# U with one 512-column matmul for a key's high part, halves summed on VectorE, and a quarter of the low parts on GpSimd

## Chip, cores and metric

One core of one Trainium2 chip runs the whole kernel. The metric is device microseconds of one execution. The profile is one further execution, taken with the hardware profiler; its span runs from the first to the last instruction.

## The reference

One decoder layer in fp32 for 256 tokens of width 1024: a mixer, cross-attention, and then the PEER channel mixer, which this change is about. Cut to that:

```python
q = (t @ w_q).reshape(T, PEER_HEADS, 2, PEER_HALF)
s = jnp.einsum('thpd,hpnd->thpn', q, sub_keys)
s_top, i_top = lax.top_k(s, PEER_TOPK)
...
best_s, pos = lax.top_k(cand_s, PEER_TOPK)
ids = jnp.take_along_axis(cand_i, pos, axis=-1)
gates = jax.nn.softmax(best_s, axis=-1)
...
act = jax.nn.gelu(jnp.einsum('td,ted->te', x_c, u[ids_c]), approximate=False)
return jnp.einsum('te,ted->td', g_c * act, v[ids_c])
```

There are 128 x 128 experts. The kernel does not gather rows of u and v. It computes gelu(x u) for every expert, multiplies by a routing matrix that is zero outside the chosen ones, and multiplies by all of v.

## The kernel before

**Precision.** fp32 operands are split in two fp32r parts: the high part is a copy of the value into fp32r (made by ScalarE, ACT), the low part is the value minus the high part (made by VectorE, DVE). A product is then three matmuls: high x high, high x low and low x high.

**Stages.** The mixer and cross-attention run to about 298 us. The U stage runs over 128 keys; for one key j the product of 128 experts (rows) with 256 tokens is made, over 8 chunks of 128 of the model width. That is 24 matmuls of 256 columns a key (L1214 to L1216), into `bank[k][:, 0:T]` with k = j % 4. Then come the routing stage (groups of 4 tokens, L1243 on TensorE) and the V stage (L1262, 512-column matmuls, 12 a key).

**Buffers of U.** `raw` holds two halves of two keys each; SP loads a half (1 MB, L261) once DVE has made the low parts of both its keys (`s_ul`). `hl`, `hl2` and `hl3u` are four slots for the high and low parts, one for each k. The tokens' high and low parts lie side by side in `xt[:, c, 0]` and `xt[:, c, 1]`. There are four PSUM banks, one for each k.

**Order of the U stage.** Each engine has its own queue, written by hand, and goes through it in order.
- TensorE (PE): key j waits for its low part (`s_ul`) and for the gelu of key j-4, which frees its bank (`s_ua`).
- ACT, in a loop of 8 keys: `gelu(j)` reads the bank and writes `act_w[:, j]` (L581); then `split_high` (L577) makes the high part of key j+4, once PE is done with key j and the data has landed.
- DVE, written out without a loop: `split_low` (L886) for key j+4, and then, for some keys, one `route_pass`. A route pass is a quarter of the top-16 search for one of 16 pairs of token tile and head: parts 0 and 1 find the best 16 of 128 scores (L902 to L910), part 2 the best 16 of 256 candidates (L912, L902 to L906), part 3 turns positions to indices (L917 to L926). There are 64 of them, spread by `5 * (j + 1) // 8 > parts`, which gives 5 in 8 keys.
- GpSimd (POOL) does nothing in U. Its subtraction of 128x2048 in two earlier weight units (L312) and its work in the routing stage (L320, L327) are the places where it runs beside DVE.
- At the end, inside the last four keys, PE transposes the routing rows `krow` (L1222) into the unused half of banks 0 to 2 and ACT copies each to `kt3` (L607), from which routing starts.

## Time and profile before

| | us |
|---|---|
| median of 3 runs | 1159.22 |
| lowest and highest | 1153.96, 1159.23 |
| span of the profiled execution | 1152.3 |
| U stage in it, first to last matmul | 300.6 to 670.4 |
| routing stage | 670.4 to 798 |
| V stage | 798 to 1146.6 |

No own time of the profiled execution is given beside its span; the median is 6.9 us longer than the span. The time of an engine's instruction can be read in two ways: its duration, and the step from its start to the start of the next one in the queue, which is shorter where the next one had nothing to wait for.

### The profile page before, as it was taken

The page shows a single profiled execution, that of the slowest core. Times are in us where ns is not written, and L with a number is a line of the kernel's source. Part 1 is how long each engine was busy: PE and PEld are TensorE (multiplying, and loading weights), DVE is VectorE, ACT ScalarE, POOL GpSimd, SP SyncE. Part 2 cuts the span into 40 slices and gives each one's busy share as a digit, 9 for nine tenths or more (in the row PEclk, how much of TensorE's full clock was granted, in tenths as well). Part 3 has the DMA queues.
Part 4 walks back from the last instruction along what each step waited for, and adds up shares of the span by engine and source line. Part 5 has one row for each costly group of instructions (what it writes and reads, how often), then busy time and mean ns, then how long its engine had stood idle before and what let it go on. Part 6 is the DMA issues. An engine that isn't in the chain of part 4 may idle for free.

```text
span 1152.3 us, 20363 instructions
## 1 busy us (share of the span) xinstructions
PE 1085.2 (94%) x7278; PEld 1002.3 (87%) x7278; DVE 786.0 (68%) x1333; ACT 621.2 (54%) x1034; POOL 120.7 (10%) x101
## 2 busy tenths in 40 slices
PE   7999999989999999999999976667999999999998
PEld 6988999889899999999999975656888888888886
DVE  5774674453488889888884489998555555555554
ACT  6775555453555555555555576665545545455453
POOL 0000110010000000000000067884000000000000
PEclk9999999999999999999999988898999999999999
DMA  9544345252355454555445520001555555555552
GB/s 318 167 149 145 111 167 163 74 183 110 112 181 184 180 184 180 182 184 182 183 180 185 185 86 0 0 0 36 188 204 191 185 198 200 182 191 207 184 187 105
DMA packets 60658, 179.54 MB, mean 156 GB/s; under 512 B 4048, under 2 KB 42960, under 8 KB 44112
## 3 DMA queue, kind: packets, MB, share of 16 engines
q1 hardware_dynamic: 60624, 179.09, 44.7%
q8 instruction: 21, 0.34, 0.1%
q14 instruction: 13, 0.11, 0.0%
HBM read 178.03 MB, written 1.05 MB: 155 GB/s over the span
## 4 chain that ended last, share of the span: by engine, by line
PE 48%; issue 40%; DVE 7%; ACT 2%; POOL 2%; DMA 1%; DVEq 0%; POOLq 0%; SPq 0%; ACTq 0%
PE acc L1262 30%; PE acc L1044 13%; PE bank L1243 2%; DVE act_w L968 2%; DVE oh_i L957 2%; DVE oh_j L957 1%; POOL oh_i L320 1%; ACT wsp L347 1%; DVE wsp L663 1%; DMA wraw<-w_in 1%; PE bank L1148 0%; PE bank L1126 0%; POOL sqd L327 0%; PE bank L1073 0%; POOL wsp L312 0%
## 5 line engine op out<-in xcount | busy, mean ns | idle before, releaser
L886 DVE TENSOR_TENSOR hl<-raw,hl 128x1024 fp32r<-128x1024 f32 x192 | 234.4, 1225 | 170.0 <-ACT hl L577 168.2
L577 ACT ACTIVATE hl<-raw 128x1024 fp32r<-128x1024 f32 x192 | 202.6, 1056 | 135.7 <-PE acc L1262 126.3
L1262 PE MATMUL acc<-hl,whl 128*128 128x512 f32 x1152 | 266.6, 389 | 1.8 <-DVE whl L985 1.8
L1262 PEld LDWEIGHTS acc<-hl,whl 128*128 128x128 f32 x1152 | 216.3, 188 | 46.6 <-issue 1.9
L1214 PE MATMUL bank<-xt,hl 128*128 128x256 f32 x768 | 218.1, 284 | 0.0
L1215 PE MATMUL bank<-xt,hl 128*128 128x256 f32 x768 | 217.5, 283 | 0.0
L1216 PE MATMUL bank<-xt,hl 128*128 128x256 f32 x768 | 217.5, 283 | 0.0
L1214 PEld LDWEIGHTS bank<-xt,hl 128*128 128x128 f32 x768 | 147.5, 192 | 0.3 <-DVE hl L886 0.3
L1215 PEld LDWEIGHTS bank<-xt,hl 128*128 128x128 f32 x768 | 147.6, 192 | 0.2 <-issue 0.2
L1216 PEld LDWEIGHTS bank<-xt,hl 128*128 128x128 f32 x768 | 147.5, 192 | 0.0
L663 DVE TENSOR_TENSOR wsp<-wraw,wsp 128x2048 fp32r<-128x2048 f32 x35 | 80.2, 2290 | 73.9 <-ACT wsp L347 73.7
L581 ACT ACTIVATE act_w<-bank 128x256 f32 (+1 forms) x128 | 48.9, 382 | 144.4 <-PE bank L1216 139.9
L1243 PE MATMUL bank<-oh_j,oh_i 128*128 128x128 f32 x512 | 86.2, 330 | 39.8 <-POOL oh_i L320 39.7
L1044 PE MATMUL acc<-xt,wsp 128*128 128x256 f32 x960 | 119.0, 287 | 3.5 <-DVE xt L684 3.5
L1044 PEld LDWEIGHTS acc<-xt,wsp 128*128 128x128 f32 x960 | 117.6, 194 | 4.5 <-issue 4.3
L1243 PEld LDWEIGHTS bank<-oh_j,oh_i 128*128 128x128 f32 x512 | 77.2, 234 | 48.7 <-issue 38.9
L347 ACT ACTIVATE wsp<-wraw 128x2048 fp32r<-128x2048 f32 x35 | 66.9, 1913 | 81.8 <-PE acc L1044 81.8
L1262 PE MATMUL acc<-hl3v,whl 128*128 128x512 f32 x384 | 92.4, 389 | 0.0
L1262 PEld LDWEIGHTS acc<-hl3v,whl 128*128 128x128 f32 x384 | 72.1, 188 | 14.9
L320 POOL TENSOR_TENSOR oh_i<-oh_i,kt 128x512 f32<-128x512 f32 x64 | 80.7, 1271 | 22.3 <-DVE oh_i L957 22.3
L1214 PE MATMUL bank<-xt,hl3u 128*128 128x256 f32 x256 | 72.6, 284 | 0.0
L1215 PE MATMUL bank<-xt,hl3u 128*128 128x256 f32 x256 | 72.5, 283 | 0.0
(207 smaller groups left out, 1448.3 us busy)
## 6 DMA issues: line engine op xcount, KB each, us to landing
raw<-u_t SPq DMA_DIRECT2D x64, 1024.0 KB, 4.8
raw<-v SPq DMA_DIRECT2D x64, 1024.0 KB, 4.7
wraw<-w_in SPq DMA_DIRECT2D x9, 1024.0 KB, 8.0
wraw<-w_pq SPq DMA_DIRECT2D x8, 1024.0 KB, 5.2
wraw<-w_ck SPq DMA_DIRECT2D x4, 1024.0 KB, 5.0
wraw<-w_cv SPq DMA_DIRECT2D x4, 1024.0 KB, 4.9
wraw<-w_out SPq DMA_DIRECT2D x4, 1024.0 KB, 4.9
wraw<-w_cq SPq DMA_DIRECT2D x4, 1024.0 KB, 5.0
```

What stands on the lines that cost most here:

```text
L320: nc.gpsimd.tensor_tensor(oh_i(slot), oh_i(slot), kt3[:, 2, ds(t0, GRP)].unsqueeze(2).broadcast_to([P, GRP, P]), ALU.mult).then_inc(s_gi, 1)
L347: nc.scalar.activation(wsp[:, u % 2, 0], wraw[:, u % WRAW], ACT.Copy).then_inc(s_wh, 1)
L577: nc.scalar.activation(eslot(k, 0, second), raw[:, k // 2, k % 2], ACT.Copy).then_inc(ready, 1)
L581: nc.scalar.activation(act_w[:, ds(j, 1)].rearrange("p o t -> p (o t)"), bank[k % 4][:, 0:T], ACT.Gelu).then_inc(s_ua, 1)
L663: V.tensor_tensor(wsp[:, u % 2, 1], wraw[:, u % WRAW], wsp[:, u % 2, 0].bitcast(F32), ALU.subtract).then_inc(s_wl, 1)
L886: V.tensor_tensor(eslot(k, 1, second), raw[:, k // 2, k % 2], eslot(k, 0, second).bitcast(F32), ALU.subtract).then_inc(ready, 1)
L1044: last = pe.matmul(dst, a, b, start=(c == c0 and n == 0), stop=(c == c1 - 1 and n == 2))
L1214: pe.matmul(bank[k][:, 0:T], uh[:, c], xt[:, c, 0], start=(c == 0), stop=False)
L1215: pe.matmul(bank[k][:, 0:T], uh[:, c], xt[:, c, 1], start=False, stop=False)
L1216: last = pe.matmul(bank[k][:, 0:T], ul[:, c], xt[:, c, 0], start=False, stop=(c == DC - 1))
L1243: last = pe.matmul(bank[slot][:, P * k:P * k + P], oh_i(slot)[:, k], oh_j(slot)[:, k], start=True, stop=True)
L1262: last = pe.matmul(acc[:, 2 * t + n], a, b[:, 512 * n:512 * n + 512], start=False, stop=last_key and k == 2, skip_group_check=True)
```

## The change

Four things.
- PE: in place of two 256-column matmuls with the same weights (high part of the key against the tokens' high part, then their low part), one matmul of 512 columns takes both (`xt[:, c]` is contiguous). The low part of the key still meets the tokens' high part in 256 columns. A key has 16 matmuls.
- The two halves of the bank must be added. ACT copies the right half to `act_w[:, j]` (`half_out`), DVE adds the left half to it (`u_sum`), and ACT makes the gelu for two keys at once in SBUF (`gelu_pair`, 512 columns). A bank is free after `u_sum` (`s_us`).
- The low part of every key with k = 3 is made by POOL (`u_low`, `s_ulp`); DVE makes the other three. SP waits for both before it loads the half of keys 2 and 3. Route passes are spread 3 in 5 keys.
- The whole bank is in use, so the transposes of `krow` and the copies to `kt3` now follow after the last key.

```diff
--- before.py
+++ after.py
@@ -172,6 +172,7 @@
         s_oi, s_gi, s_dif, s_ojd, s_oja, s_sqd, s_gm, s_gw = (sem(n) for n in (
             "s_onehot_i", "s_gated_i", "s_differences", "s_onehot_j_dve", "s_onehot_j_act", "s_sq_distance", "s_route_mm", "s_route_mul"))
         s_seed = sem("s_seed")
+        s_us, s_u2, s_ulp, s_kt = sem("s_u_sum"), sem("s_u_half_out"), sem("s_u_low_pool"), sem("s_key_cols_mm")
         s_vh, s_vl, s_Wh, s_Wl, s_vm = (sem(n) for n in ("s_v_high", "s_v_low", "s_a_high", "s_a_low", "s_v_mm"))
         s_fs, s_fv, s_fd, s_fin = (sem(n) for n in ("s_fin_squares", "s_fin_var", "s_fin_dev", "s_fin"))
 
@@ -257,10 +258,14 @@
                 sp.dma_start(raw[:, q], u_t[q]).then_inc(s_raw[q], 16)
             with sp.Fori(1, KEYS // 4) as it:
                 for q in range(2):
-                    sp.wait_ge(s_ul, it * 4 - 4 + 2 * q + 2)
+                    sp.wait_ge(s_ul, it * 3 - 3 + q + 2)
+                    if q:
+                        sp.wait_ge(s_ulp, it)
                     sp.dma_start(raw[:, q], u_t[ds(it * 2 + q, 1)].rearrange("o p j d -> (o p) j d")).then_inc(s_raw[q], 16)
             for q in range(2):
-                sp.wait_ge(s_ul, KEYS - 4 + 2 * q + 2)
+                sp.wait_ge(s_ul, 3 * (KEYS // 4) - 1 + q)
+                if q:
+                    sp.wait_ge(s_ulp, KEYS // 4)
                 sp.dma_start(raw[:, q], vd[q]).then_inc(s_raw[q], 16)
             sp.wait_ge(s_um, KEYS)
             sp.dma_start(gfin[:], g_final.rearrange("(o d) -> o d", o=1).broadcast_to([P, D])).then_inc(s_gf, 16)
@@ -312,6 +317,15 @@
                 nc.gpsimd.tensor_tensor(wsp[:, u % 2, 1], wraw[:, u % WRAW], wsp[:, u % 2, 0].bitcast(F32),
                                         ALU.subtract).then_inc(s_wlp, 1)
 
+
+            def u_low(n):
+                pool.wait_ge(s_uh, n)
+                nc.gpsimd.tensor_tensor(eslot(3, 1, False), raw[:, 1, 1], eslot(3, 0, False).bitcast(F32),
+                                        ALU.subtract).then_inc(s_ulp, 1)
+
+            u_low(4)
+            with pool.Fori(1, KEYS // 4) as it:
+                u_low(it * 4 + 4)
 
             pool.wait_ge(s_kte, 3)
 
@@ -576,35 +590,45 @@
                     act.wait_ge(*free)
                 nc.scalar.activation(eslot(k, 0, second), raw[:, k // 2, k % 2], ACT.Copy).then_inc(ready, 1)
 
-            def gelu(j, k):
+            def half_out(j, k):
                 act.wait_ge(s_um, j + 1)
-                nc.scalar.activation(act_w[:, ds(j, 1)].rearrange("p o t -> p (o t)"), bank[k % 4][:, 0:T], ACT.Gelu).then_inc(s_ua, 1)
+                nc.scalar.activation(act_w[:, ds(j, 1)].rearrange("p o t -> p (o t)"), bank[k % 4][:, T:2 * T],
+                                     ACT.Copy).then_inc(s_u2, 1)
+
+            def gelu_pair(j):
+                act.wait_ge(s_us, j + 2)
+                aw = act_w[:, ds(j, 2)]
+                nc.scalar.activation(aw, aw, ACT.Gelu).then_inc(s_ua, 1)
 
             act.wait_ge(s_pv, HEADS + CHEADS)
             for k in range(4):
                 split_high(k, 16 if k % 2 == 0 else None, (s_seed, 1) if k == 2 else None, s_uh)
             base16 = 16 * (KEYS // 4)
 
-            with act.Fori(0, KEYS // JPB - 1) as it:
+            for it in range(KEYS // JPB - 1):
                 for jj in range(JPB):
                     j = it * JPB + jj
                     if jj == JPB - 1:
                         act.wait_ge(s_rt, it + 1)
-                    gelu(j, jj)
-
+                    half_out(j, jj)
                     split_high(jj % 4, (it * 2 + (jj // 4 + 2)) * 16 if jj % 2 == 0 else None, (s_um, j + 1), s_uh)
+                    if jj % 2:
+                        gelu_pair(j - 1)
 
             act.wait_ge(s_rt, TT * PH)
             nc.scalar.activation(krow[:, 2], krow[:, 2], ACT.Exp).then_inc(s_ge, 1)
             for jj in range(JPB):
                 j = KEYS - JPB + jj
+                half_out(j, jj)
                 if jj < 4:
                     split_high(jj, base16 if jj % 2 == 0 else None, (s_um, j + 1), s_uh)
                 elif jj < 7:
                     split_high(jj - 4, base16 + 16 if jj % 2 == 0 else None, (s_um, j + 1), s_vh, second=True)
-                gelu(j, jj)
-                if 4 <= jj < 7:
-                    nc.scalar.activation(kt3[:, jj - 4], bank[jj - 4][:, T:2 * T], ACT.Copy).then_inc(s_kte, 1)
+                if jj % 2:
+                    gelu_pair(j - 1)
+            for k in range(3):
+                act.wait_ge(s_kt, k + 1)
+                nc.scalar.activation(kt3[:, k], bank[k][:, T:2 * T], ACT.Copy).then_inc(s_kte, 1)
 
 
             def onehots(it, n, g, t0, slot, first):
@@ -925,18 +949,23 @@
                     rlink(V.tensor_reduce(kr[:, 0:2, ds(it, 1)].rearrange("p a o k -> p a (o k)"), eq[:], X, ALU.add))
                     V.tensor_scalar(kr[:, 2, ds(it, 1)], topv[:, 2:3], topv[:, 2, 0:1], None, ALU.subtract).then_inc(s_rt, 1)
 
-            for k in range(4):
+            def u_sum(j):
+                dve.wait_ge(s_u2, j + 1)
+                V.tensor_tensor(act_w[:, j], bank[j % 4][:, 0:T], act_w[:, j], ALU.add).then_inc(s_us, 1)
+
+            for k in range(3):
                 split_low(k, s_ul, (s_uh, k + 1))
             dve.wait_ge(s_ke, 8)
 
 
             parts = 0
-            for j in range(KEYS - 1):
-                if j < KEYS - 4:
+            for j in range(KEYS):
+                u_sum(j)
+                if j < KEYS - 4 and j % 4 < 3:
                     split_low(j % 4, s_ul, (s_uh, j + 5))
-                else:
+                elif KEYS - 4 <= j < KEYS - 1:
                     split_low(j % 4, s_vl, (s_vh, j + 5 - KEYS), second=True)
-                if parts < 4 * TT * PH and 5 * (j + 1) // 8 > parts:
+                if parts < 4 * TT * PH and 3 * (j + 1) // 5 > parts:
                     route_pass(parts // 4, parts % 4)
                     parts += 1
                 if j == KEYS - JPB:
@@ -1201,33 +1230,35 @@
             last.then_inc(s_seed, 1)
 
 
-            def u_keys(it, first=False, last_pass=False):
+            def u_keys(it, first=False):
                 for k in range(4):
-                    pe.wait_ge(s_ul, it * 4 + (k + 1))
+                    if k < 3:
+                        pe.wait_ge(s_ul, it * 3 + (k + 1))
+                    else:
+                        pe.wait_ge(s_ulp, it + 1)
                     if first:
                         pe.wait_ge(s_ke, 5 + k)
                     else:
-                        pe.wait_ge(s_ua, it * 4 + (k - 3))
+                        pe.wait_ge(s_us, it * 4 + (k - 3))
                     uh = eslot(k, 0, False).rearrange("p (c i) -> p c i", c=DC)
                     ul = eslot(k, 1, False).rearrange("p (c i) -> p c i", c=DC)
                     for c in range(DC):
-                        pe.matmul(bank[k][:, 0:T], uh[:, c], xt[:, c, 0], start=(c == 0), stop=False)
-                        pe.matmul(bank[k][:, 0:T], uh[:, c], xt[:, c, 1], start=False, stop=False)
+                        pe.matmul(bank[k][:], uh[:, c], xt[:, c].rearrange("p a t -> p (a t)"), start=(c == 0), stop=False)
                         last = pe.matmul(bank[k][:, 0:T], ul[:, c], xt[:, c, 0], start=False, stop=(c == DC - 1))
-                    if last_pass and k < 3:
-
-                        if k == 0:
-                            pe.wait_ge(s_gr, 1)
-                        for t in range(TT):
-                            last = pe.transpose(bank[k][:, T + P * t:T + P * t + P], krow[:, k, t], ident[:])
                     last.then_inc(s_um, 1)
 
             u_keys(0, first=True)
-            with pe.Fori(1, KEYS // 4 - 1) as it:
+            with pe.Fori(1, KEYS // 4) as it:
                 u_keys(it)
-            u_keys(KEYS // 4 - 1, last_pass=True)
-
-            pe.wait_ge(s_ua, KEYS)
+
+            pe.wait_ge(s_gr, 1)
+            for k in range(3):
+                pe.wait_ge(s_us, KEYS - 3 + k)
+                for t in range(TT):
+                    last = pe.transpose(bank[k][:, T + P * t:T + P * t + P], krow[:, k, t], ident[:])
+                last.then_inc(s_kt, 1)
+
+            pe.wait_ge(s_ua, KEYS // 2)
             pe.wait_ge(s_kte, 3)
 
             def route(it, slot, first=False):
```

Where the new instructions stand, by the program's order. DVE, soon after the start of U (keys 4 to 6 before, 5 to 8 now). `hl`, `hl_54` and `hl3u` are the slots of the parts (L886 before, L910 now), `act_w<-bank` is the new sum, the rest are route passes. Before:

```order
L886 TENSOR_TENSOR hl<-raw,hl 128x1024
L912 TENSOR_TENSOR cand<-topv 128x256
L902 MAX topv<-cand 128x8
L903 MATCH_REPLACE candw<-topv,cand 128x256
L904 MAX topv<-candw 128x8
L905 MAX_INDEX topi<-topv,cand 128x8
L906 MAX_INDEX topi<-topv,candw 128x8
L886 TENSOR_TENSOR hl<-raw,hl 128x1024
L886 TENSOR_TENSOR hl_54<-raw,hl_54 128x1024
L917 TENSOR_SCALAR posu<-topi 128x16
```

DVE's queue now:

```order
L954 TENSOR_TENSOR act_w<-bank,act_w 128x256
L910 TENSOR_TENSOR hl<-raw,hl 128x1024
L954 TENSOR_TENSOR act_w<-bank,act_w 128x256
L910 TENSOR_TENSOR hl_54<-raw,hl_54 128x1024
L941 TENSOR_SCALAR posu<-topi 128x16
L942 TENSOR_SCALAR posu<-topi 128x16
L943 CAST posf<-posu 128x32
L944 TENSOR_TENSOR eq<-posf,iota 128x512
L947 TENSOR_TENSOR eq<-eq,topf 128x512
L949 TENSOR_REDUCE krow<-eq 128x2x16
L950 TENSOR_SCALAR krow<-topv 128x16
L954 TENSOR_TENSOR act_w<-bank,act_w 128x256 x2
```

Each key now has a sum ahead of its split, and where the key's slot is the fourth and no route pass falls on it, two sums follow each other.

ACT's queue over four keys late in U, now (L595 is the copy of the right half, L591 the high part, L601 the gelu of two keys). Before, it was L581 and L577 in turn, one of each for a key.

```order
L595 ACTIVATE act_w<-bank 128x256
L591 ACTIVATE hl<-raw 128x1024
L595 ACTIVATE act_w<-bank 128x256
L591 ACTIVATE hl<-raw 128x1024
L601 ACTIVATE act_w<-act_w 128x512
```

The gelu of two keys waits for DVE's sum, and stands ahead of the next key's copy and high part.

ACT at the end of U, before:

```order
L581 ACTIVATE act_w<-bank 128x256
L607 ACTIVATE kt_65<-bank 128x256
L581 ACTIVATE act_w<-bank 128x256
L616 ACTIVATE sqd_66<-sqd_66 128x512
L621 ACTIVATE oh_j_70<-sqd_66,ones 128x512
```

and now, where the three copies to `kt3` have moved behind the last gelu:

```order
L595 ACTIVATE act_w<-bank 128x256
L601 ACTIVATE act_w<-act_w 128x512
L631 ACTIVATE kt_65<-bank 128x256 x3
L640 ACTIVATE sqd_66<-sqd_66 128x512
L645 ACTIVATE oh_j_70<-sqd_66,ones 128x512
```

## Rows read from the trace of the kernel before

**Rows 1.** The page, 40 equal slices of the span: DVE's busy tenths.
```profile
DVE  5774674453488889888884489998555555555554
```

**Rows 2.** Busy time by stretch: length, PE, PEld, DVE, ACT, POOL (count), granted clock, DMA.
```profile
300.60:670.40 369.80, 369.80 (x3080) 369.40 (x3078) 294.65 (x678) 193.98 (x277) 1.08 (x1) 1.00 0.51 182
400.00:500.00 100.00, 100.00 (x836) 100.00 (x835) 87.68 (x217) 50.90 (x74) 0.00 (x0) 1.00 0.52 184
682.00:798.00 116.00, 77.80 (x470) 69.45 (x469) 115.01 (x135) 73.17 (x171) 91.44 (x72) 0.87 0.00 0
```

**Rows 3.** Who waited for whom from 400 to 600 us: total, times, longest.
```profile
ACT act_w L581 <- PE bank L1216: 84.3, 61, 1.6
DVE hl L886 <- ACT hl L577: 7.8, 15, 1.3
```

**Rows 4.** The chain that ended last, its piece in V: start, us, what.
```profile
798.16 348.43 PE acc L1262 x1536
```

**Rows 5.** DVE in order of time: start, duration, line, operation, [idle before].
```profile
447.78 0.42 DVE L912 TENSOR_TENSOR cand<-topv 128x256 f32<-128x256 f32 x1
...
450.60 1.23 DVE L886 TENSOR_TENSOR hl<-raw,hl 128x1024 fp32r<-128x1024 f32 x1
...
453.54 0.17 DVE L917 TENSOR_SCALAR posu<-topi 128x16 uint32<-128x16 uint32 x1
...
454.04 0.69 DVE L920 TENSOR_TENSOR eq<-posf,iota 128x512 f32<-128x512 f32 x1
454.76 0.69 DVE L923 TENSOR_TENSOR eq<-eq,topf 128x512 f32<-128x512 f32 x1
...
456.35 1.22 DVE L886 TENSOR_TENSOR hl<-raw,hl 128x1024 fp32r<-128x1024 f32 x1
457.49 0.28 DVE L902 MAX8 topv<-srow 128x8 f32<-128x128 f32 x1
...
459.39 1.22 DVE L886 TENSOR_TENSOR hl<-raw,hl 128x1024 fp32r<-128x1024 f32 x1
```

**Rows 6.** DVE before 240 us, two adds of a PSUM and an SBUF operand in succession.
```profile
231.33 0.76 DVE L831 TENSOR_TENSOR xr<-acc,xr 128x256 f32<-128x256 f32 x2 [1.46 <-PE acc L1044]
```

**Rows 7.** ACT in order of time, in U.
```profile
456.80 0.39 ACT L581 ACTIVATE act_w<-bank 128x256 f32 x1 [1.55 <-PE bank L1216]
457.08 1.05 ACT L577 ACTIVATE hl<-raw 128x1024 fp32r<-128x1024 f32 x1
459.68 0.39 ACT L581 ACTIVATE act_w<-bank 128x256 f32 x1 [1.55 <-PE bank L1216]
```

**Rows 8.** All instructions in order of time, where POOL's L312 runs beside DVE.
```profile
165.28 4.60 POOL L312 TENSOR_TENSOR wsp<-wraw,wsp 128x2048 fp32r<-128x2048 f32 x1 [24.18 <-ACT wsp L347]
...
166.67 3.75 DVE L679 TENSOR_SCALAR xs<-xr,stat 128x1024 f32<-128x1024 f32 x1
```

**Rows 9.** Single lines: duration min/median/max in ns, first and last start, form.
```profile
L679 DVE TENSOR_SCALAR xs<-xr,stat x6: 753/754/3752, 5.9 to 240.3; 128x1024 f32<-128x1024 f32 x6
```

**Rows 10.** The same view, one of DVE's lines in the routing stage, beside POOL.
```profile
L957 DVE TENSOR_TENSOR oh_i<-iota,kt x64: 678/1140/1553, 669.9 to 792.4; 128x512 f32<-128x512 f32 x64
```

**Rows 11.** The same view, POOL's line in the routing stage.
```profile
L320 POOL TENSOR_TENSOR oh_i<-oh_i,kt x64: 1034/1452/1487, 671.6 to 793.6; 128x512 f32<-128x512 f32 x64
```

**Rows 12.** The page, DMA issues: count, KB each, median us to landing.
```profile
raw<-u_t SPq DMA_DIRECT2D x64, 1024.0 KB, 4.8
```

**Rows 13.** The end of U in order of time: POOL.
```profile
669.32 1.54 POOL L327 TENSOR_TENSOR sqd<-kt,iota 128x512 f32<-128x512 f32 x1 [431.34 <-ACT kt L607]
```

**Rows 14.** The same stretch, DVE.
```profile
669.88 5.02 DVE L957 TENSOR_TENSOR oh_i<-iota,kt 128x512 f32<-128x512 f32 x4
```

**Rows 15.** The same stretch, ACT.
```profile
668.87 0.38 ACT L607 ACTIVATE kt<-bank 128x256 f32<-128x256 f32 x1
670.45 0.38 ACT L581 ACTIVATE act_w<-bank 128x256 f32<-128x256 f32 x1 [1.21 <-PE bank L1216]
670.95 0.63 ACT L616 ACTIVATE sqd<-sqd 128x512 f32<-128x512 f32 x1
```

## The prediction, made before the changed kernel was run

> **What bounds the kernel now.** First the chain of waits and the busy shares by stretch. In the U stage (369.8 us, a third of the span) TensorE (PE) is busy without a gap at a granted clock of 1.00, its upper level of 2.4 GHz [rows 2]. The waits say the same from the other side: of the waits in 200 us of U, ScalarE (ACT) waits 84.3 us for PE, VectorE (DVE) 7.8 us for ACT, and PE waits for nobody [rows 3]. ACT starts a gelu every 2.88 us, once a key, each time after 1.55 us of waiting for PE [rows 7]. So U lasts 128 keys of PE: 369.5 / 128 = 2.887 us a key, 24 matmuls, 120.3 ns each.
>
> Then see who is next. DVE is at 88% between 400 and 500 us [rows 2] and at 8 tenths in most slices of U [rows 1]. Its queue, in steps from start to start [rows 5]: a split takes 1.14 us (456.35 to 457.49), route parts 0 and 1 1.90 us (457.49 to 459.39), part 2 2.82 (447.78 to 450.60), part 3 2.81 (453.54 to 456.35). A round of four parts is 9.43 us. Per 20 keys that is 20 x 1.14 + 12.5 x 9.43/4 = 22.8 + 29.5 = 52.3 us of 57.7. DVE hides behind PE with 5 us in 58 to spare. After routing ends, at about key 102, DVE has room.
>
> **PE's part.** The V stage shows what a 512-column matmul costs: 348.43 us for 1536 of them [rows 4], 226.8 ns. Against two of 256 columns, 240.6 ns, it saves 13.8 ns. A key becomes 8 x (226.8 + 120.3) = 2.777 us, U becomes 355.5 us: **14.0 us less**, if nothing but PE sets the pace. Both ends: at the least nothing is saved (a 512 followed by a 256 in other weights does not occur in the trace), and no row supports more than 14. I take 14, since both kinds run back to back at the full clock and show the same 13 to 14 ns over their columns at 2.4 GHz.
>
> On this the Trainium skill's page VectorE: DVE Perf Modes (section The TRN2 errata) differs: it gives a matmul 6 cycles over its columns, 2.5 ns, by which the 1024 matmuls fewer would be worth an estimated 2.6 us. The rows here disagree with that figure by a factor of five, and the rows are used.
>
> **DVE's part.** Removed: 5 of 20 splits, 5.7 us. The route spread of 3 in 5 gives 12 parts in 20 keys, 28.3 us. Added: 20 sums of a PSUM half and an SBUF row. The nearest row adds the same operands in the same shape: two in 0.76 us, each 0.42 with a step of 0.34 [rows 6]. Taken at 0.34: 6.8 us; at 0.42 it would be 8.4. The sum: 17.1 + 28.3 + 6.8 = **52.2 us in 20 keys, where PE now needs 55.5**. The reserve falls from 5.4 to 3.3 us. Two things eat it.
>
> *The handshake with ACT.* `gelu_pair` of an odd key waits for DVE's sum and stands ahead of the next key's copy and high part. While PE sets the pace this is free. Once DVE is late, each odd key makes DVE wait for ACT: 0.1 for the signal, 0.53 for a gelu of 512 (the nearest row, a 512-element SBUF square, takes 0.63 [rows 15]), 0.38 for the copy and 0.1: the next sum can start 1.1 us after the last, and the next split at 0.1 + 0.53 + 0.28 + 1.05 + 0.1 = 2.06 us [rows 7]. Where a route pass stands between, it hides that. In 20 keys the odd ones without a pass are 5, 7, 15 and 17. At 5 and 17 DVE has a split (1.14) and a sum (0.34) to do and waits 0.6; at 7 and 15, where the split has gone to POOL, it waits 1.1 and then 0.6. Together **4.6 us**.
>
> *The port.* POOL now reads and writes SBUF during U. The trace shows what this does to DVE. L312 on POOL takes from 165.28 to 169.88; a DVE instruction started at 166.67 takes 3.75 us and ends at 170.42, 0.54 us after POOL's [rows 8], where the same line takes 0.75 alone [rows 9]. It was held until POOL was through. Instructions with two SBUF operands are held too: L957 takes 0.68 alone, 1.14 in the median and 1.55 at most in the routing stage, and POOL's own L320 goes from 1.03 to 1.45 [rows 10, 11]. A split, the cand of part 2 and both eq of part 3 have two SBUF operands; the sum has one.
>
> The Trainium skill, SBUF — State Buffer (section Who interferes with whom), states this as an exclusive lock: a DVE instruction with two SBUF inputs and a GpSimd one that reads SBUF block each other for the whole instruction. The trace agrees, by the 3.75 us.
>
> A low part of 1024 on POOL, by 4.60 us for 2048 and 1.03 for 512 [rows 8, 11], takes 1.03 + (4.60 - 1.03)/3 = 2.2 us. Five of them in 20 keys can hold DVE for 0 to 11 us. To see how much, I wrote the queues of 20 keys out, with these durations and DVE late. One of the five as an example: ACT has the high part for key 11's slot ready just as DVE, behind with its work, begins part 3 for key 6; POOL takes the port 0.2 us into it, the first eq is due 0.3 us later and waits for the rest of POOL's 2.2 us, 1.9 us, and everything behind it in DVE's queue moves by as much. The five fall so: ahead of a split, but there DVE is first (0.2 us lost, at a cast); just at the start of part 3, both eq wait (1.9); after a split and ahead of part 2, whose cand waits (1.9); behind part 3, the next split waits (1.4); inside a cand (0). Together **5.4 us**, half of the most.
>
> **The sum.** DVE late, 20 keys take 52.2 + 4.6 + 5.4 = 62.2 us, against 57.7 before and 55.5 for PE. So PE comes to wait for DVE's low parts. Through key 106, with the last route part (2.8 us) off the path: 107/20 x 62.2 - 2.8 = 330.0. Plus 4 us for the first dozen keys, where DVE has nothing to fall behind on and waits as it does now (12% of 2.9 us a key, and the first sum only behind key 0). Then PE does keys 110 to 127 at its own pace, 18 x 2.777 = 50.0. U is 384.0, **14.5 more than 369.5**.
>
> *The tail.* Before, the copies to `kt3` lay inside the last keys (the last at 668.87), POOL started routing at 669.32 and DVE at 669.88, ahead of PE's end at 670.4 [rows 13 to 15]. Now DVE's first one-hot waits for the half copy (0.5 after PE), the sum (0.4), the gelu (0.6) and the first of three copies (0.5): 2.0 after PE's end instead of 0.5 ahead. POOL's start moves by about 3.5. DVE is busy 99% of routing [rows 2], so its shift is what counts: **+2.7** (1.5 to 3.5). V is not touched.
>
> *At nothing:* ACT's table load, one a loop turn before, is now rare, and ACT has 1.55 us a key idle (costs nothing unless ACT becomes late). ACT's added work: a copy for a gelu, and half a gelu of 512, 0.3 us a key. SP's load of the second half waits for POOL: POOL's end, landing 4.8 [rows 12], two high parts and a copy, 2.2 of POOL make 10.4 us per 4 keys, under the 11.1 of PE's pace; held by a split it is 11.5, still under the 12.4 above.
>
> Total: 1152.3 + 14.5 + 2.7 = 1169.5 us of span; with the 6.9 us that the median stands above the profiled span, **1176 us, 1.5% slower**.
>
> **The rivals.**
> 1. *PE stays the bound (faster).* If DVE is held little, since POOL starts when ACT finishes a high part and DVE, being on time, is in a sum or a maximum then. 52.2 + 4.6 = 56.8 in 20 keys is then hardly above PE's 55.5. U 355.5 to 358, tail 2.7: 1148 to 1151 us. For: the reserve of 3.3, and an on-time DVE splits key 4 only after POOL's 2.2 us are over. Against: once a part 3 or a cand meets POOL, 2 us are lost, and the handshake keeps it late.
> 2. *Halfway.* Each us of port loss in 20 keys is worth 107/20 = 5.35 in the total. Even with before is U = 369.5 - 2.7 = 366.8, so (366.8 - 50.0 - 4 + 2.8)/5.35 = 59.0 for 20 keys, a loss of 2.2 us. That is the point from which the change is slower. Losses of 1.1 to 3.3 us give 1153 to 1165.
> 3. *Port dearer.* A loss of 8 us or more, as when each POOL instruction stands before a split: 5.35 x 2.6 = 14 more, 1190 and up. Also if the sum costs 0.42 with a gap each: +8.
> 4. *The 512-column matmul doesn't save:* by itself +14 on rival 1, so 1162; under my forecast DVE sets the pace and only the last 18 keys lose 2 us.
>
> **How the numbers follow.** A measurement here tells 0.5% (5.8 us) from no change. My forecast, 1165 to 1188: 0.52. Rival 1 (with up to 1.1 us of port loss, to 1153): 0.24. Rivals 2 and 4: 0.14. Rival 3: 0.10. The time is the forecast's, 1176. The range reaches to 1149 and 1190, leaving out the lowest of rival 1 and most of rival 3. Faster 0.24, same 0.14, slower 0.62.
>
> **What would show it.** Right: PE waits in U for L910 or L323, about 10% of the time up to key 110, DVE at 95% or more with splits and eq lasting up to 3 us where POOL runs, ACT waiting for the sum at L601, and a pace of 3.0 to 3.1 us a key that falls to 2.78 after routing. Wrong: PE without gaps at 2.78 us a key (rival 1), splits of 1.2 us beside POOL (no port), or a sum of well over 0.4 us. A granted clock under 1.00 in U, from PE's waits, would add what none of these sums has.

## The result: slower by 2.7%, and the profile after

The changed kernel takes 1188.23 us in the median of 4 runs (1184.45 to 1190.87), the kernel before 1158.19 (1153.96 to 1159.23). The ratio is 1.0267, with a 95% interval of 1.023 to 1.0304. The profiled execution took 1190.61 us, with a span of 1188.7. One of the six executions in experiment 9 below took 1224.87 us at a mean granted clock of 0.839, against 0.975 to 0.985 in the other five, and its ratio leaves it out.

The stages by the trace: U runs from 304.0 to 704.1 us, that is 400.1 us, where it was 369.6 (both to the last matmul's start plus its 0.12 us; the 369.8 of the table ahead goes to its modelled end). Routing and the gap ahead of V take 130.4 us (704.1 to 834.5) where they took 127.9. From V's first matmul to the end of the span it is 354.2 us, as before.

The page of the changed kernel, DVE and POOL by slices, with the granted clock. It answers to [rows 1].

```profile
DVE  5775674442688999999999569999555555555554
POOL 0000010000121121112112138887000000000000
PEclk9989999999999999999999998889999999999999
```

DVE was at 8 tenths in most slices of U and is now at 9, where POOL shows its 1 or 2 tenths. Busy time by stretch (length, PE, PEld, DVE, ACT, POOL, clock, DMA) answers to [rows 2]:

```profile
400.00:500.00 100.00, 91.58 (x495) 77.64 (x494) 90.95 (x216) 47.25 (x78) 19.43 (x8) 0.97 0.44 158
```

PE was busy all the time and is now idle 8% of it. Who waited for whom from 400 to 600 us answers to [rows 3]:

```profile
ACT act_w L601 <- DVE act_w L954: 102.6, 31, 5.8
PEld bank L1246 <- issue: 24.2, 21, 2.8
PE bank L1246 <- DVE hl L910: 14.5, 13, 2.5
DVE hl L910 <- ACT hl L591: 5.8, 12, 0.5
DVE act_w L954 <- ACT act_w L595: 5.8, 6, 1.0
```

ACT used to wait for PE; it now waits for DVE's sum, half of the time (102.6 us of 200). PE waits for DVE's low parts; part of PE's waiting stands under "issue", since the profile finds no releaser for it. DVE waits for ACT in 11.6 us of 200. DVE sets the pace, together with its waits for ACT.

What happens in its queue is in DVE's order of time:

```profile
441.57 0.42 DVE L954 TENSOR_TENSOR act_w<-bank,act_w 128x256 f32<-128x256 f32 x1
441.91 3.35 DVE L910 TENSOR_TENSOR hl<-raw,hl 128x1024 fp32r<-128x1024 f32 x1
445.19 0.41 DVE L954 TENSOR_TENSOR act_w<-bank,act_w 128x256 f32<-128x256 f32 x1
...
455.48 2.27 DVE L943 CAST posf<-posu 128x32 f32<-128x32 uint32 x1
457.78 0.69 DVE L944 TENSOR_TENSOR eq<-posf,iota 128x512 f32<-128x512 f32 x1
...
460.10 0.42 DVE L954 TENSOR_TENSOR act_w<-bank,act_w 128x256 f32<-128x256 f32 x1
461.49 0.42 DVE L954 TENSOR_TENSOR act_w<-bank,act_w 128x256 f32<-128x256 f32 x1 [0.97 <-ACT act_w L595]
462.44 1.23 DVE L910 TENSOR_TENSOR hl<-raw,hl 128x1024 fp32r<-128x1024 f32 x1 [0.52 <-ACT hl L591]
...
469.20 3.33 DVE L910 TENSOR_TENSOR hl<-raw,hl 128x1024 fp32r<-128x1024 f32 x1
...
481.70 3.34 DVE L910 TENSOR_TENSOR hl<-raw,hl 128x1024 fp32r<-128x1024 f32 x1
```

and POOL's, a little further on:

```profile
441.79 2.39 POOL L323 TENSOR_TENSOR hl3u<-raw,hl3u 128x1024 fp32r<-128x1024 f32 x1 [8.36 <-ACT hl3u L591]
455.32 2.38 POOL L323 TENSOR_TENSOR hl3u<-raw,hl3u 128x1024 fp32r<-128x1024 f32 x1 [11.14 <-ACT hl3u L591]
469.09 2.37 POOL L323 TENSOR_TENSOR hl3u<-raw,hl3u 128x1024 fp32r<-128x1024 f32 x1 [11.38 <-ACT hl3u L591]
481.56 2.40 POOL L323 TENSOR_TENSOR hl3u<-raw,hl3u 128x1024 fp32r<-128x1024 f32 x1 [10.10 <-ACT hl3u L591]
495.87 2.56 POOL L323 TENSOR_TENSOR hl3u<-raw,hl3u 128x1024 fp32r<-128x1024 f32 x1 [11.90 <-ACT hl3u L591]
506.79 2.40 POOL L323 TENSOR_TENSOR hl3u<-raw,hl3u 128x1024 fp32r<-128x1024 f32 x1 [8.37 <-ACT hl3u L591]
```

POOL started at 441.79, 0.12 us ahead of DVE's split. The split lasts 3.35 us where it takes 1.22, and ends 1.08 us after POOL's 444.18, about its own length. A cast of 32 elements lasts 2.27 us where it takes 0.18 (455.48). The pattern repeats after 65.0 us (441.79, 506.79), that is 20 keys: 3.25 us a key, where PE needed 2.887 before. Over these 65.0 us: 52.2 us of DVE's work, three splits held 2.1 us each (441.91, 469.20, 481.70) and one cast 2.1, together 8.4, and 3.9 us of waiting for ACT (0.97 twice, 0.52 twice, 0.45 twice). That makes 64.5.

The end of U, in DVE's and ACT's order of time, answers to [rows 14, 15]:

```profile
706.14 4.18 DVE L986 TENSOR_TENSOR oh_i<-iota,kt 128x512 f32<-128x512 f32 x4 [0.97 <-ACT kt L631]
```

```profile
705.21 0.63 ACT L601 ACTIVATE act_w<-act_w 128x512 f32<-128x512 f32 x1 [0.49 <-DVE act_w L954]
705.74 0.91 ACT L631 ACTIVATE kt<-bank 128x256 f32<-128x256 f32 x3
```

DVE starts routing 2.0 us after PE's end at 704.1; it started 0.5 us ahead of it.

### The profile page after: what moved, and what is told of

Same layout as the page of the kernel before. It is cut to its first block, busy times and chain, and to the rows that moved or that the text cites. A ratio compares the mean times of both kernels' runs of the same rounds, so it can differ in the third digit from the quotient of the medians.

```text
span 1188.7 us, 18325 instructions
## 1 busy us (share of the span) xinstructions
PE 1091.1 (92%) x6254; PEld 952.3 (80%) x6254; DVE 833.8 (70%) x1429; ACT 631.7 (53%) x1084; POOL 198.3 (17%) x133
## 4 chain that ended last, share of the span: by engine, by line
PE 47%; issue 41%; DVE 7%; ACT 2%; POOL 2%; DMA 1%; DVEq 0%; POOLq 0%; SPq 0%; ACTq 0%
PE acc L1293 29%; PE acc L1073 12%; PE bank L1274 2%; DVE act_w L997 2%; DVE oh_i L986 2%; DVE oh_j L986 1%; ACT wsp L361 1%; DMA wraw<-w_in 1%; POOL oh_i L334 1%; DVE wsp L687 1%; PE bank L1177 0%; PE bank L1155 0%; PE bank L1102 0%; POOL wsp L317 0%; DVE xs L703 0%
## 5 line engine op out<-in xcount | busy, mean ns | idle before, releaser
L910 DVE TENSOR_TENSOR hl<-raw,hl 128x1024 fp32r<-128x1024 f32 x192 | 262.8, 1369 | 148.7 <-ACT hl L591 148.7
L1246 PE MATMUL bank<-xt,hl 128*128 128x512 f32 x768 | 280.4, 406 | 21.3 <-DVE hl L910 20.7
L591 ACT ACTIVATE hl<-raw 128x1024 fp32r<-128x1024 f32 x192 | 202.8, 1057 | 133.7 <-PE acc L1293 126.2
L1247 PE MATMUL bank<-xt,hl 128*128 128x256 f32 x768 | 218.1, 284 | 0.0
L1246 PEld LDWEIGHTS bank<-xt,hl 128*128 128x128 f32 x768 | 147.0, 191 | 64.2 <-issue 29.7
L1247 PEld LDWEIGHTS bank<-xt,hl 128*128 128x128 f32 x768 | 147.9, 193 | 0.2 <-issue 0.2
L323 POOL TENSOR_TENSOR hl3u<-raw,hl3u 128x1024 fp32r<-128x1024 f32 x32 | 77.8, 2430 | 378.9 <-ACT hl3u L591 378.9
L601 ACT ACTIVATE act_w<-act_w 128x512 f32<-128x512 f32 x64 | 40.4, 632 | 167.7 <-DVE act_w L954 167.7
L1246 PE MATMUL bank<-xt,hl3u 128*128 128x512 f32 x256 | 91.6, 398 | 5.0 <-DVE act_w L954 5.0
L954 DVE TENSOR_TENSOR act_w<-bank,act_w 128x256 f32<-128x256 f32 x128 | 53.9, 421 | 26.0 <-ACT act_w L595 24.3
L1247 PE MATMUL bank<-xt,hl3u 128*128 128x256 f32 x256 | 71.7, 280 | 0.0
```

The costliest lines, as they stand in the source:

```text
L323: nc.gpsimd.tensor_tensor(eslot(3, 1, False), raw[:, 1, 1], eslot(3, 0, False).bitcast(F32), ALU.subtract).then_inc(s_ulp, 1)
L591: nc.scalar.activation(eslot(k, 0, second), raw[:, k // 2, k % 2], ACT.Copy).then_inc(ready, 1)
L910: V.tensor_tensor(eslot(k, 1, second), raw[:, k // 2, k % 2], eslot(k, 0, second).bitcast(F32), ALU.subtract).then_inc(ready, 1)
L954: V.tensor_tensor(act_w[:, j], bank[j % 4][:, 0:T], act_w[:, j], ALU.add).then_inc(s_us, 1)
L1246: pe.matmul(bank[k][:], uh[:, c], xt[:, c].rearrange("p a t -> p (a t)"), start=(c == 0), stop=False)
L1247: last = pe.matmul(bank[k][:, 0:T], ul[:, c], xt[:, c, 0], start=False, stop=(c == DC - 1))
```

## The experiments

In all of them the pace is read from the distance of route passes or low parts that are 20 keys apart in the steady part of U. The lines of code differ from kernel to kernel by a few numbers. The ratios are to the kernel before, which was run again beside each group of experiments (medians 1157.4 to 1158.5 us).

**1. DVE makes all low parts.** POOL's `u_low` and its waits are out, PE and SP wait for `s_ul` alone:

```diff
-                if j < KEYS - 4 and j % 4 < 3:
+                if j < KEYS - 4:
                     split_low(j % 4, s_ul, (s_uh, j + 5))
```

> The changed kernel with POOL's part undone: DVE makes all low parts again, everything else stays. My theory (DVE sets the pace; in 20 keys of the changed kernel's steady stretch 52.2 us of work, 8.4 us of being held by POOL and 3.9 us of waiting for ACT): DVE's work rises by 5 splits of 1.14 us to 57.9, the 8.4 go, the waits for ACT shrink to about 2.4 since keys 7 and 15 have a split again: 60 us in 20 keys against 65. U about 373 us instead of 400, total near 1163 us, between before and the changed kernel. Rival (the port is a side show, DVE is simply overbooked by the sums and the handshake): 5.7 us more work in 20 keys make it slower than the changed kernel, 1205 us or more.

1166.25 us (ratio 1.0075, 1.0049 to 1.0101), against 1188.23. U is 376.5 us; 20 keys take 59.9 us (route passes whose last instruction starts at 450.88 and at 510.80). More work for DVE made the kernel 22 us faster. So it is not overbooking alone; in this queue what POOL's help costs is more than the 5.7 us in 20 keys that it saves.

**2. POOL's quarter alone, in the kernel before.** Matmuls, gelus and the end of U as before; POOL's `u_low` and the waits for it as in the changed kernel.

```diff
-                if j < KEYS - 4:
+                if j < KEYS - 4 and j % 4 == 3:
+                    pass
+                elif j < KEYS - 4:
                     split_low(j % 4, s_ul, (s_uh, j + 5))
```

> The kernel before with POOL's part alone: POOL makes the low part of each fourth key, the matmuls, gelus and transposes are as before. My theory: DVE has 46.6 us of work in 20 keys and may be held 11 us at most, under the 57.7 us of PE, so PE stays the bound and the time is that of before, 1158 us within 4; DVE's instructions beside POOL still show 2 us of holding. Rival (POOL as the maker of a low part is too slow, by its 2.4 us or through the load of the second half that waits for it): slower by itself, 1165 us or more.

1155.34 us, ratio 0.9989 (0.9972 to 1.0005): no difference. U is 369.6 us, as before. Busy time in its U:

```profile
400.00:500.00 100.00, 100.00 (x836) 100.00 (x835) 90.16 (x217) 51.40 (x73) 20.78 (x9) 1.00 0.52 186
```

PE has no gap. DVE is busier than before (90.16 against 87.68) with fewer splits, since it is held; here mostly in a cast of 16 elements, 0.76 us in the mean where it takes 0.17:

```profile
L924 DVE CAST topf<-topi 128x16 f32<-128x16 uint32 x22 | 16.7, 758 | 0.8
```

(line, engine, operation, count, busy us, mean ns, idle before). The holding is there, and costs nothing while PE is the bound.

**3. Without the sum.** ACT makes the gelu straight from the left half of the bank; the 512-column matmuls and POOL's share stay. The kernel leaves out the product of the keys' high parts with the tokens' low parts, so it is a probe and no candidate.

```diff
-                nc.scalar.activation(act_w..., bank[k % 4][:, T:2 * T], ACT.Copy).then_inc(s_u2, 1)
+                nc.scalar.activation(act_w..., bank[k % 4][:, 0:T], ACT.Gelu).then_inc(s_us, 1)
...
-                u_sum(j)
```

> The changed kernel with the sum of the halves left out (ACT makes the gelu from the left half of the bank, one key at a time as before; so the product with the tokens' low parts is computed but not used in the result): 16 matmuls a key and POOL's low parts stay. My theory: DVE's work is 45.4 us in 20 keys, plus at most 11 us held, near PE's 55.5; PE sets the pace nearly everywhere and shows what the matmul change is worth: U 355.5 to 360 us, total 1146 to 1150 us. Rival (the 512-column matmul saves only 2 to 3 us): 1158 us.

1143.48 us (0.988, 0.985 to 0.9909). **4. The same, with all low parts on DVE:**

> As the run without the sum, and DVE makes all low parts (POOL idle in U). My theory: DVE's work is 51.1 us in 20 keys, PE sets the pace without any holding: U 355.5 us, total 1146 us, and PE's period is 2.777 us a key. If DVE held by POOL matters even without the sum, this is faster than that run by some us; if not, the two are equal.

1147.07 us (0.9896, 0.9864 to 0.9928). U is 355.3 us in both, where 355.5 was worked out. The two medians differ by 3.6 us, but not in U: of the 4.8 us between the two spans 1.9 lie ahead of U (it starts at 303.3 in one and 305.2 in the other, with the stages before it unchanged) and 2.8 behind V's first matmul. In each PE is busy without a gap; the stretch from experiment 3:

```profile
400.00:500.00 100.00, 100.00 (x579) 88.19 (x578) 88.41 (x214) 49.24 (x72) 22.40 (x9) 1.00 0.52 188
```

So the 512-column matmul gives its 14 us, and U's loss against these runs comes in with the sum, that is with its work on DVE, the waits between DVE and ACT that it brings, and with POOL's holding, which costs nothing while PE is the bound. Experiments 5 to 8 tell these three apart.

**5. The gelu of a pair four keys later,** so that ACT never waits for a fresh sum; POOL's share stays.

```diff
-                    if jj % 2:
-                        gelu_pair(j - 1)
+                    if jj % 2 and j > 3:
+                        gelu_pair(j - 5)
```

> The changed kernel with the handshake undone: the gelu of a pair stands four keys later in ACT's queue, so it never waits for a sum just made; POOL's low parts stay. My theory: the 3.9 us in 20 keys in which DVE waits for ACT go, the sum of work and holding by POOL stays: 52.2 + 8.4 = 60.6 us against 65, total about 1188 - 5.35 x 4.4 = 1165 us; as POOL now starts at other points of DVE's queue, the holding can fall anywhere from 3 to 11 us, so 1150 to 1180. Rival (ACT's waits are only a symptom): no change, 1188 us.

1159.11 us, ratio 1.0014 (0.9995 to 1.0034): 29 us less than the changed kernel, and no different from the kernel before. U is 370.2 us, 20 keys take 58.5. DVE's waits for ACT are gone from its groups in 400 to 600 us, and the holding has moved:

```profile
L912 DVE TENSOR_TENSOR hl<-raw,hl 128x1024 fp32r<-128x1024 f32 x51 | 67.6, 1325 | 0.0
L956 DVE TENSOR_TENSOR act_w<-bank,act_w 128x256 f32<-128x256 f32 x68 | 28.0, 420 | 1.0
L938 DVE TENSOR_TENSOR cand<-topv 128x256 f32<-128x256 f32 x11 | 13.4, 1219 | 0.0
L952 DVE TENSOR_SCALAR krow<-topv 128x16 f32<-128x16 f32 x10 | 7.5, 754 | 0.4
```

Over their lengths alone (1.22, 0.42, 0.23, and 0.17 for the cast, which takes 6.5 us in 20) these are held 22.4 us in 68 keys, 6.6 us in 20. The handshake thus cost its own 3.9 us and about 2 more, since POOL now starts at other points of DVE's queue and holds it less (6.6 us for 8.4).

**6. Late gelu and all low parts on DVE.** Both edits together.

> The 512-column matmuls and the sum, DVE making all low parts, and the late gelu: both causes removed. My theory: DVE's work of 57.9 us in 20 keys is all that is left, against 55.5 for PE: U about 5.35 x 57.9 + 51 = 361 us, total 1152 us, a little under before and 14 under the run with the low parts on DVE. Rival (the handshake costs nothing once POOL is gone): as that run, 1166 us.

1163.01 us, ratio 1.0041 (1.0025 to 1.0056). This missed: 1152 was expected, and the rival's 1166 is nearer. 20 keys take 58.8 us (450.07 to 508.89), not 57.9, and U 372.5 instead of 361. The 11.5 us are 4.8 of pace (107/20 x 0.9), 4.2 in the first keys (the last route pass ends at 626.8, 304.0 + 107 x 2.94 + 8.2, where 4 was taken) and 2.5 in the last (52.5 us from the end of the last low part ahead of that pass to PE's end at 676.5, for 50.0). In the first keys DVE waits for ACT's high part once for 2.8 us (its split at 311.25), and ACT waits for route rows for 5.1 us up to 330.81. The 0.9 us of pace are one wait of DVE in 20 keys, 0.93 us at 481.04 and as long, within 0.1, at 422.22, 539.89 and 598.71; ACT, on whom it waits, makes the high part from 479.94 on, after 4.62 us of its own waiting for the load, which was issued at 475.10:

```profile
481.04 1.23 DVE L900 TENSOR_TENSOR hl<-raw,hl 128x1024 fp32r<-128x1024 f32 x1 [0.93 <-ACT hl L579]
```

With no POOL and no handshake, then, DVE's own 57.9 us in 20 keys are still more than PE's 55.5, and its waits for the load come on top. And the late gelu is worth 3 us here (1166.25 to 1163.01), where it was worth 29 with POOL's share in.

**7. POOL beside DVE, with nothing to deliver.** The kernel of experiment 1, and on POOL two subtractions of 512 elements that nobody waits for until the end of U.

```diff
+            for g in range(1, KEYS // 4 + 1):
+                pool.wait_ge(s_uh, 4 * g)
+                for _ in range(2):
+                    pool.wait_ge(s_pool, beside)
+                    bc = iota[:].unsqueeze(1).broadcast_to([P, GRP, P])
+                    nc.gpsimd.tensor_tensor(kt3[:, 0:2]..., bc, bc, ALU.subtract).then_inc(s_pool, 1)
+                    beside += 1
```

> The run with the low parts on DVE, and beside it POOL does work that nobody needs and nobody waits for, where its low part stood: two subtractions of 512 elements, two SBUF inputs each, about 2.1 us in all. Nothing of U depends on them. Theory of the port: DVE is held as in the changed kernel, 5 to 8 us in 20 keys, 1190 to 1205 us. Rival (what cost time was the wait for POOL's result, not the port): 1166 us as without it.

1189.1 us (1.0285, 1.026 to 1.031), 23 us over experiment 1, and 65.0 us for 20 keys. U is 402.2. Until the end of U nothing waited for POOL's results. By the trace DVE's instructions last 5.0 us longer in 20 keys than in experiment 1, and 59.9 + 5.0 is the 65 measured. The holding is the cause. The split, in the single-line view:

```profile
L908 DVE TENSOR_TENSOR hl<-raw,hl x192: 1208/1226/2010, 302.6 to 1169.6; 128x1024 fp32r<-128x1024 f32 x192
```

It is held 0.8 us at most, by POOL instructions of half the length (1.04 us where DVE does not hold them); casts, the eq of part 3 and a few others are held too.

**8. The same with writes only.** Four memsets of 512 elements in place of the subtractions.

> As the run with POOL's useless subtractions, but with four memsets of 512 elements in their place, which write SBUF and read nothing. If the port that is shared is the one for reading, instructions of DVE with two SBUF operands aren't held, only casts and scalar operations may be: 1166 to 1170 us. If any work of POOL holds DVE, the splits are held for up to its length and the time goes up by a share of it, 1175 us or more.

1169.99 us (1.0116, 1.0099 to 1.0133), 3.7 us over experiment 1, with intervals that touch; 20 keys take 60.7 us for 59.9. The split is never held, a cast at times:

```profile
L907 DVE TENSOR_TENSOR hl<-raw,hl x192: 1212/1226/1227, 299.3 to 1147.2; 128x1024 fp32r<-128x1024 f32 x192
```

```profile
L940 DVE CAST posf<-posu x16: 181/182/557, 325.2 to 629.4; 128x32 f32<-128x32 uint32 x16
```

POOL was busy 17.44 us in 100, nearly the changed kernel's 19.43, and splits did run beside it: the one at 459.22 starts 0.14 us behind a memset (459.08 to 459.61) and lasts 1.22. So in these kernels an instruction with two SBUF operands is held by POOL's subtractions, which read and write, and not by its memsets, which only write. The cast is held by both.

**9. Route passes over 120 keys,** late gelu, all low parts on DVE.

```diff
-                if parts < 4 * TT * PH and 3 * (j + 1) // 5 > parts:
+                if parts < 4 * TT * PH and (8 * (j + 1) + 4) // 15 > parts:
```

> The run with low parts on DVE and the late gelu, and the route passes spread over 120 keys (8 in 15) instead of 107 (3 in 5). DVE's work in 20 keys falls from 57.9 us (58.0 measured there) to 22.8 + 6.8 + 10.67 x 2.36 = 54.8 us, under PE's 55.5. My theory (all that counts is DVE's sum against PE's): PE sets the pace, U 356 to 360 us instead of 372.5, total 1147 to 1151 us. Rival (something else than DVE's sum keeps that run at 1163, for one the start of U): 1160 us or more.

1151.57 us, ratio 0.9948 (0.9929 to 0.9966). U is 362.9 us and the time 1151.57, both a little over what was expected; from 400 to 600 us PE is busy all the time (200.00 us of 200). Three us less work for DVE in 20 keys gained 11 us, and DVE's sum came under PE's.

**10. The same, with the last four keys in the form of before,** the gelu of these from the bank, the transposes and copies inside the keys.

```diff
+                        if last_pass:
+                            pe.matmul(bank[k][:, 0:T], uh[:, c], xt[:, c, 0], start=(c == 0), stop=False)
+                            pe.matmul(bank[k][:, 0:T], uh[:, c], xt[:, c, 1], start=False, stop=False)
+                        else:
                             pe.matmul(bank[k][:], uh[:, c], xt[:, c]..., start=(c == 0), stop=False)
```

> As the run with the spread passes, and the last four keys in the form of before: three 256-column matmuls, the gelu from the bank, the transposes of the route rows in the bank's free half inside the keys, the copies to kt3 between them. It gives back 32 x 13.8 ns = 0.4 us of matmul time and takes the tail away, 2.5 us by the traces of the changed kernel (DVE starts routing 2.0 us after PE's end, 0.5 before it in the kernel before): 2 us under the run with the spread passes, 1145 to 1149 us, faster than both kernels. If the tail hides elsewhere, equal to that run.

1150.35 us, ratio **0.9937 (0.9923 to 0.9952)**: the fastest that computes the whole result, 0.6% below the kernel before, and over the 1145 to 1149 expected. Against experiment 9 it is 1.2 us in the medians, whose intervals overlap: the tail's 2.5 us are not told apart there. In the two traces U's end to V's first matmul is 127 us against 131, but this stretch differs by 2 us also between the kernel before and experiment 2, whose ends of U are alike.

**11. POOL's share kept, late gelu, route passes over 120 keys.**

> The changed kernel with POOL's low parts kept, the late gelu and the route passes spread over 120 keys. DVE's work in 20 keys is 17.1 + 6.8 + 25.2 = 49.1 us, and it can be held 11 us at most; at the 6.6 us held in the run with the late gelu it makes 55.7 us, on PE's 55.5. My theory: U 356 to 362 us, 1148 to 1154 us, about like the run with all low parts on DVE: POOL's share takes 5.7 us of work from DVE and costs about as much in holding. Rival (POOL's help is worth its 5.7 us): 2 us or more faster than that run; (the holding grows to its full 11): 60 us in 20 keys, 1165 us.

1162.03 us (1.0039, 1.0023 to 1.0056), 10 us over experiment 9, from which it differs by POOL's share alone. It lies between what was expected and the rival of full holding. DVE's groups from 400 to 600 us:

```profile
L912 DVE TENSOR_TENSOR hl<-raw,hl 128x1024 fp32r<-128x1024 f32 x52 | 80.7, 1551 | 2.4 <-ACT hl L591 2.0
L938 DVE TENSOR_TENSOR cand<-topv 128x256 f32<-128x256 f32 x9 | 8.0, 890 | 0.0
L936 DVE CAST topf<-topi 128x16 f32<-128x16 uint32 x19 | 6.4, 339 | 0.7
```

Held in these three: 17.3 + 4.2 + 3.1 = 24.6 us in 69 keys, 7.1 in 20, against 5.7 saved. PE besides waited for POOL itself here, 3.9 us in U. But at 3 passes in 5 keys, experiments 5 and 6, the kernel with POOL's share was 4 us faster than the one without (2.3 of them in U). There DVE set the pace either way, and the holding, 6.6 us, about balanced the 5.7 of work saved and the 0.9 us of wait that fell away; at the wider spread PE sets the pace when POOL is out, and taking work from DVE gains nothing. What POOL's share is worth thus hangs on where its instructions fall and on how much reserve DVE has, from 22 us lost (experiment 1 against the changed kernel) to 4 gained.

## Why the prediction was right, and where its sizes were off

The direction, the mechanism and the order of the causes held: 1176 was forecast, 1188.23 came, inside 1149 to 1190 and just above the forecast case (1165 to 1188). The change itself, 17 us by the sum, came out as 30 in the medians and 36 in the two spans. That the time lay inside the range is in part luck: 5 us that did not belong in the base stood in for a part of what the port's term lacked, and without them the same range would have ended at 1185.

- **PE's part, 14.0 us.** Right to 0.2 us: U is 355.3 us in the runs without the sum. The 6 cycles over the columns that the Trainium skill's page VectorE: DVE Perf Modes gives in The TRN2 errata (an estimated 2.6 us in all) do not hold for these matmuls.
- **DVE's work, 52.2 us in 20 keys.** Right: the sum takes 0.42 us with steps of 0.34 (441.57 to 441.91), and with POOL gone 20 keys take 59.9 us, where 60 was expected; with the handshake gone too they take 58.8, of which 0.9 is a wait, which leaves the 57.9 of the sum with all splits on DVE.
- **The handshake, 4.6 us.** 3.9 measured, the waits at the places named: 1.0 and 0.5 at the two odd keys with neither split nor pass, 0.45 at the others. Its indirect part, that it fixes where POOL starts, was not in the working; taking it away gave 29 us, not the 23 expected, and only 3 where POOL had no share.
- **The port, 5.4 us.** This is the term that was too small: 8.4 measured. The step that failed is the list of the five places. It had DVE first at a split; the trace has POOL first at three splits in 20 keys, by 0.1 us. At part 3 the cast is held, and not the eq behind it. Of the 16.1 us by which U came out longer than forecast (400.1 against 384.0), the pace makes 5.35 x (65.0 - 62.2) = 15.0: 3.0 us more holding in 20 keys, 0.7 less handshake, and 0.5 for which no row accounts. POOL's low part takes 2.4 us, where 2.2 was worked out. The prediction put the 3.75 us of L679 beside the rule of the Trainium skill (SBUF — State Buffer, Who interferes with whom) for instructions with two SBUF inputs, but L679 is a TENSOR_SCALAR with one input tensor. For two inputs the rule, that one side blocks the other for the whole instruction, is borne out by the split's 3.35 us.
- **The tail, 2.7 us.** 2.5 by the trace, both in DVE's first one-hot (2.0 behind PE's end for 0.5 ahead) and in the stretch from U to V (130.4 for 127.9).
- **The time around the span.** The 6.9 us put on the span were wrong. The changed kernel's profiled execution took 1190.61 us with a span of 1188.7: 1.9 around it. The profiled execution of before must then have been near 1154, the lowest of its runs. On spans, 1169.5 was forecast and 1188.7 came, 19.2 more: 16.0 in U, 3.4 because U started later (304.0 against 300.6), and 0.2 less in the tail. This start lies from 300.6 to 305.2 in the thirteen kernels profiled, which have the same stages ahead of it, and is not the change's.
- **The rivals.** That PE stays the bound fell: it did so only where DVE had less to do, in the runs without the sum and in experiments 9 and 10. The dearer port (8 us or more) is what came, by its condition, though its time of 1190 was just missed. The terms for the first and the last keys, 4 and 50.0 us, measured 3.5 and 51.7, 1.2 more together, about the rest of the 16.1: the last route pass ends at 655.2, which is 304.0 + 107 x 3.25 + 3.5, and from 2.8 us ahead of that it is 51.7 to 704.1.
- **At nothing.** ACT's waits for `raw` (6.3 us in U) and its table loads stayed hidden, as said. The granted clock was 0.97 from 400 to 500 us, in a stretch in which PE was idle 8% of the time, where 1.00 was taken; in experiment 1, with PE idle 4.5%, it was 1.00. DVE set the pace, so no cost of it shows.

## What to carry to other kernels

Before an edit moves work off the bounding engine, add up the queue of the next engine in the same units, waits for its partners included: here 14 us on PE left DVE 3.3 us of reserve in 55.5, and 12.3 us of holding and waiting came on top. Work given to POOL may cost DVE as much as it saves if it reads SBUF while DVE has casts or instructions with two SBUF operands in its queue: count each POOL instruction as up to its own length on DVE, and test by letting it do nothing useful. A wait for a fresh result belongs as far back in the queue as buffers allow. And causes that meet in one queue do not add up: four keys' delay of the gelu was worth 29 us with POOL's share in and 3 without, and POOL's share lost 22 us with the early gelu and gained 4 with the late one.

## What the runs showed of the hardware

- A cast of 16 or 32 elements on DVE is held by POOL's whole instruction like a long one: 2.27 us for 0.18 (changed kernel), 0.76 in the mean for 0.17 (experiment 2).
- POOL's memsets of 0.53 us did not hold DVE's splits, which have two SBUF operands (1.227 us at most in all of them, experiment 8), but its subtractions did (3.35 us beside one of 2.4, 2.06 beside those of 1.04).
- Matmuls of 512 and of 256 columns in turn, each in its own weights, take 347.0 ns a pair (355.3 us for 1024 pairs, experiments 3 and 4), the sum of the 226.8 and 120.3 ns that each kind takes by itself.
- Three splits that start 0.11 to 0.14 us behind POOL's instruction, and a cast 0.16 us behind it, cost 2.1 us each, and the pattern comes back every 20 keys, from 395 us on the same to 0.1 us.
